# A chunked state-space scan: ScalarE makes the next chunk's first decay whole at the end of a chunk

## The reference

```
cs = cumsum(ac)                          # ac = dt * A, per head
seg = cs[:, :, None] - cs[:, None, :]
lmat = exp(where(causal, seg, -inf))     # the decay between two tokens of a chunk
cb = einsum("blgn,bsgn->blsg", cc, bc)
y_diag = einsum("blsg,blsgj,bsgjp->blgjp", cb, lmat, xc)
y_off = einsum("blgn,bgjpn,blgj->blgjp", cc, state, exp(cs))
new_state = state * exp(cs[:, -1]) + einsum("blgn,blgj,blgjp->bgjpn", bc, decay, xc)
```

## Time and profile before

| | us |
|---|---|
| median of three runs | 2900.41 (2899.1 to 2905.93) |
| the profiled execution, its own time | 2911.98 |
| its span | 2910.1 |
| busy in the span: PE / PEld | 2810.4 (97%) / 2375.7 (82%) |
| busy: DVE / ACT / POOL | 1589.1 (55%) / 1240.7 (43%) / 1583.0 (54%) |

### The profile page before, as it was taken

One profiled execution on the slowest core, in us unless ns is written; L12 is line 12 of the kernel. 1 busy time (PEld: TensorE's weight loads), 2 busy tenths in 40 slices (PEclk: granted clock), 3 DMA queues, 4 the chain that ended last, 5 costly groups with the idle time before them and its releaser, 6 DMA issues. The chain is left out here.

```text
span 2910.1 us, 40604 instructions
## 1 busy us (share of the span) xinstructions
PE 2810.4 (97%) x14222; PEld 2375.7 (82%) x14222; DVE 1589.1 (55%) x2525; ACT 1240.7 (43%) x2258; POOL 1583.0 (54%) x1078
## 2 busy tenths in 40 slices
PE   6999999999999999999998999999999988999998
PEld 5888888888877888888887788888999967788787
DVE  6335235896534346865424555555766675753433
ACT  5232234333234443332324556555767754542332
POOL 7677778777777688777763454452111244422000
PEclk8999999999999999999999999999999989999999
DMA  4557346532235265332345455554566388865543
GB/s 123 147 159 227 115 129 167 128 111 81 72 91 191 88 176 138 109 95 65 87 130 163 143 175 158 165 172 159 171 195 172 105 245 257 270 212 165 181 151 108
DMA packets 462802, 436.06 MB, mean 150 GB/s; under 512 B 60736, under 2 KB 403008, under 8 KB 454976
## 3 DMA queue, kind: packets, MB, share of 16 engines
q1 hardware_dynamic: 460352, 425.79, 49.1%
q0 software_dynamic: 2304, 8.39, 0.7%
HBM read 290.99 MB, written 143.13 MB: 149 GB/s over the span
## 5 line engine op out<-in xcount | busy, mean ns | idle before, releaser
L531 PE MATMUL p_acc<-h_kept,w_hi 128*128 128x512 f32 x1216 | 477.7, 393 | 5.0 <-ACT work L577 3.2
L533 PE MATMUL p_acc<-h_kept,w_lo 128*128 128x512 f32 x1216 | 475.5, 391 | 0.0
L532 PE MATMUL p_acc<-h_kept,w_hi 128*128 128x512 f32 x1216 | 474.2, 390 | 0.0
L417 POOL TENSOR_TENSOR w_lo<-p_sums,w_hi 128x512 fp32r<-128x512 f32 x300 | 395.2, 1332 | 136.2 <-ACT w_hi L618 136.2
L618 ACT ACTIVATE w_hi<-p_sums 128x512 fp32r<-128x512 f32 x300 | 189.3, 632 | 477.3 <-PE p_acc L533 454.8
L531 PEld LDWEIGHTS p_acc<-h_kept,w_hi 128*128 128x128 f32 x1216 | 228.9, 188 | 54.6 <-ACT work L577 3.4
L533 PEld LDWEIGHTS p_acc<-h_kept,w_lo 128*128 128x128 f32 x1216 | 228.9, 188 | 49.9
L532 PEld LDWEIGHTS p_acc<-h_kept,w_hi 128*128 128x128 f32 x1216 | 229.1, 188 | 48.6
L531 PE MATMUL p_acc<-p_ops,w_hi 128*128 128x512 f32 x608 | 241.9, 398 | 5.9 <-DVE p_ops L719 5.9
L533 PE MATMUL p_acc<-p_ops,w_lo 128*128 128x512 f32 x608 | 240.1, 395 | 0.0
L532 PE MATMUL p_acc<-p_ops,w_hi 128*128 128x512 f32 x608 | 238.3, 392 | 0.0
(11 more groups left out here) (343 smaller groups left out, 6795.3 us busy)
## 6 DMA issues: line engine op xcount, KB each, us to landing
raw<-w_in SPq DMA_DIRECT2D x100, 512.0 KB, 5.2
s_qs<-p_stage SPq DMA_DIRECT2D x96, 256.0 KB, 4.0
work<-s_gates SPq DMA_DIRECT2D x48, 512.0 KB, 7.3
p_rawb<-w_in SPq DMA_DIRECT2D x38, 512.0 KB, 4.0
keep<-w_in SPq DMA_DIRECT2D x38, 512.0 KB, 5.3
s_xbc<-p_stage SPq DMA_DIRECT2D x32, 512.0 KB, 2.6
work<-s_xbc SPq DMA_DIRECT2D x16, 1024.0 KB, 7.2
spare<-s_qs SPq DMA_DIRECT2D x16, 1024.0 KB, 6.1
```

Source lines behind the costliest of these rows:

```text
L417: tt(w_lo[:, k], weight(u, k), w_hi[:, k], ALU.subtract).then_inc(w_made, 1)
L531: pe.matmul(bank, hi, ops[k][:, 0, c], start=c == 0, stop=False)
L532: pe.matmul(bank, hi, ops[k][:, 1, c], start=False, stop=False)
L533: last = pe.matmul(bank, lo, ops[k][:, 0, c], start=False, stop=c == 3)
```

## The change

Three places in ScalarE's program. At the end of a chunk `falls` of the next chunk becomes `decays`, which is `falls` and then `decay`: the Exp of the next chunk's group 0 now stands behind its Relus and ahead of the chunk's third item. At the start of a chunk the Exp is gone. Ahead of the loop the first chunk's `falls` becomes `decays` too.

```
                         act.activation(b_tok[:], ps_m[:, :BANK], ACT.Copy).then_inc(b_tok_ready, 1)
-                        decay(c, 0)
                         decays(c, k, i, 1)
...
                         act.activation(std[:], ss[:], ACT.Sqrt, bias=eps[:], scale=1.0 / GW).then_inc(std_made, 1)
                         if not (last_pair and k):
-                            falls(c + 1, 1 - k, i + k, 0)
+                            decays(c + 1, 1 - k, i + k, 0)
                         take_item(3 * k + 2)
...
-                falls(0, 0, 0, 0)
+                decays(0, 0, 0, 0)
                 with act.Fori(0, PAIRS - 1) as i:
```

## The result

The changed kernel takes 2909.54 us (median of 22 runs, 2899.23 to 2923.8) against 2901.59 us of before in the same sessions (22 runs, 2897.55 to 2914.92): ratio 1.0022, 95% interval [1.0013, 1.0031]. It is slower by 0.22%, some 6 us (the plain difference of the two medians is 8.0), where I forecast 2 us less; the median lies above the range of 2891 to 2908.

A forecast was written before the change was run, and what follows sets the result against it. TensorE, busy 97% of the span, was taken to bound the kernel. Summing -12 + 2.0 + 1.1 + 0.5 + 6.8 gave -1.6, say -2 us: 2898 from a median of 2900.41, range 2891 to 2908.

The forecast's parts named there:

- The gain at group(0): TensorE's delay for the moved Exp goes: 7.6 us in eight chunks, 0.5 in chunk 1, 1.25 in even chunks 4 to 12.
- The mix bound by xdt: VectorE's group(0) mix, issued when cbm is done, ends 0.55 us after GpSimd's xdt, with 1 us in hand.
- Group(3): Its mix finishes before GpSimd's cast begins, so stalls in chunks 3, 4, 5, 9, 11 go: 2.7 us gained.
- Late copies: ScalarE's keep copies at odd chunks' ends, in chunks 5 to 15, come late and delay TensorE: 2.0 us lost.
- The sum without meetings: Gains of 12 us less 2.0 late copies, 1.1 late yn in chunks 12 and 14, 0.5 for chunk 0's Exp.
- The table load: At the chunk's end, Exp starts 1.30 us after load start; rival, 2.7 us switch by skill rule: 2914, chance 0.02.
- the price of a meeting: Odd chunks' yn under GpSimd's second split: two at 2.7 us, four meeting the cast alone at 0.45, less 0.4: 6.8 us.
- The edge: Odd chunks: a second cast starting under 0.8 us behind the first yn pushes the fourth yn instruction into GpSimd's subtraction.
- y + xd is drawn out: Issued earlier, inside GpSimd's first split, y + xd takes 0.3 to 0.7 us off the yn chain's slack.
- collisions in nearly all: Rival: five or six odd chunks' yn fall over the edge, 16 us in place of 6.8; +7.6, 2908 us; chance 0.18.

The follow-up runs named there:

- guard_after: The changed kernel with GpSimd's second split of odd chunks made to wait until VectorE has made yn; 2892.26 us, 0.9957 of before.
- guard_before: The kernel of before with GpSimd's second split of odd chunks made to wait until VectorE has made yn; 2900.44 us, 0.9985 of before.
- after_again: The changed kernel run once more, unedited; 2908.45 us, 1.0017 of before.
- collide_before: The kernel of before with the second split's weights transferred one item earlier and the split held until the square root, forcing it onto yn; 2921.53 us, 1.0063.
- early: The changed kernel with the next chunk's group 0 Relus and Exp moved up behind group 3's Exp; 2903.51 us, 1.0008 of before.
- early_guard: The kernel early plus GpSimd's second split waiting for yn; 2888.74 us, 0.995 of before.
- early_guard2: The kernel early_guard with the first split of each chunk also made to wait for y + xd; 2885.87 us, 0.994 of before.
- half_even: The changed kernel with the Exp kept at the end of even chunks alone, so only odd chunks begin without it; 2910.39 us, 1.0028 of before.
- half_odd: The changed kernel with the Exp kept at the end of odd chunks alone, so only even chunks begin without it; 2898.49 us, 0.9994 of before.

## Why the prediction was wrong

- The gain at group(0), 7.6 + 0.5 + 1.25 us: right. In both profiles of the changed kernel the distance from the z transposes to group(0) is 0.87 or 0.88 us in every chunk from 1 on; the sum of what it exceeded that by in before, 9.8 us, is gone.
- The mix bound by xdt, ending 0.55 us behind it: right, to the hundredth in chunk 3. The lock that the Trainium skill, "SBUF — State Buffer", section "Who interferes with whom", describes is what the traces show: in ten of the twelve profiles y + xd meets the first split's subtraction, 98 times in all; it is issued 0.04 to 1.9 us into it and ends 1.1 us behind it each time (alone it takes 1.22), while the subtraction takes 2.38 to 2.41 us however early y + xd comes.
- Group(3), 2.7 us: right where the clock is high. In the changed kernel it is on time in chunks 3, 4, 5, 9 and 11; it is late by 0.8 and 0.4 us (from group(0) to L1196) in chunks 10 and 12, each behind a meeting and its slow clock.
- Late copies, 2.0 us: right in kind, 3.8 us in guard_after.
- The sum without meetings: -12 + 2.0 + 1.1 + 0.5 = -8.4 us. guard_after less guard_before measures -8.2. That the two agree to 0.2 us is in part luck: the late copies alone were 1.8 us dearer, TensorE's waits for yn in guard_after are 2.1 us against 1.1, and the two intervals leave 4 to 5 us of room.
- The table load: it takes 1.28 us right behind the Relus, the Exp starts 1.29 behind its start, and there is no drain of 1.38 us as the Trainium skill, "ScalarE: Activation LUTs", section "What ACT_TABLE_LOAD costs", has it. That rival was rightly low. (By its own terms, +17 on -2, it comes to 2915, not 2914.)
- The step that failed is the price of a meeting in the term of 6.8 us: "2.7 us each", with "at 2.7 us I expect none" of the clock's falls. The edge is where I put it: over the same 42 chunks 14 have a distance under 0.8 us, and each of these has an excess of 2.8 us or more; the other 28 have 0.9 at most. The count was nearly right too: of the six chunks 3 to 13 I had two fall over it, and three do in either profile of the changed kernel (3, 9 and 11; 7, 9 and 13). Chunk 1, which I left where it was, escapes in the one and meets in the other. What a meeting costs was wrong. The clock falls behind 3.04 and 2.67 us in the changed kernel (not behind 2.77 in chunk 3), and behind 2.86, 2.94, 3.16 and 2.80 us in after_again; the head of the next chunk is then stretched by up to 2 us, and its group(3) can wait as well.

The price is read from the starts of L1166, over the chunk of the meeting and the next. After_again, chunks 9 and 11:

```profile
1803.32 1.04 PE L1166 MATMUL s_psx<-ident,work 128*128 128x128 f32 x8
...
1866.82 1.04 PE L1166 MATMUL s_psx<-ident,work 128*128 128x128 f32 x8
```

These two chunks take 63.5 us, where two undisturbed ones take 55.0: 8.5 us for one meeting. The other six of the two profiles cost 3.2 (chunk 3 of the changed kernel, where the clock stays) and 4.9 to 5.7. The trace of before had this price in it already. Its chunks 1 and 5 start at:

```profile
1574.83 1.04 PE L1166 MATMUL s_psx<-ident,work 128*128 128x128 f32 x8
...
1697.38 1.04 PE L1166 MATMUL s_psx<-ident,work 128*128 128x128 f32 x8
```

With chunk 3's start at 1639.65, chunks 1 and 2 take 64.8 us and chunks 3 and 4 take 57.7: 7.1 us for the meeting in chunk 1. I had read the 4.59 us of its yn and the 3.72 us of its idle, and not the length of the chunks. By the medians, in place of 6.8 us the meetings cost what guard_after and guard_before give: 16 to 19 us in the changed kernel less 3 to 4 in before, so 13 to 15.

- A smaller part of the same step: y + xd is drawn out by 0.35 to 1.2 us over its 1.23 in the odd chunks 1 to 13 of the two profiles, where I took 0.3 to 0.7.
- The time came out where the rival "collisions in nearly all" has it (2908, given a chance of 0.18), but not by its count: it had five or six of the six go over the edge at 2.7 us each, and three do, at 3.2 to 8.5. That its number fits is luck. The two things that mattered stood in my own rows: an edge with three distances within 0.2 us of it, and a clock that fell behind the one meeting in sight. I priced both as if they were settled.

What stays open: why the landings of `raw` vary by some tenths of a us from run to run, and so whether one can place them without a wait; and behind which of the idles the clock falls.

## What to carry to other kernels

A gain on one engine moves its instructions against work on another that does not move with them, here splits that start when a transfer issued long before has landed; ask of each instruction that comes earlier what now runs beside it. Where the neighbour shuts an engine out as it does here, the cost has an edge: yn's chain, with 0.8 to 0.9 us of slack, lost 2.8 to 3.9 us beyond it in the 14 meetings. Price what lies beyond the edge from the length of whole chunks, not from the idle alone. Fix the order by a wait where the held work has slack (the second split's weights are first used behind L1196 of the next chunk, some 20 us later), and the gain is kept. Look also for an idle place with the right table loaded before moving a table load.

## What the runs showed of the hardware that I had not expected

- TensorE's granted clock falls to the lower level behind idles of 1.99, 2.00 and 1.96 us in chunks 5, 7 and 11 of collide_before, and stays high behind 1.97, 1.96, 2.32 and 1.96 us in the other four. It stays high behind 3.17 us in chunk 9 of early, and behind 3.48 us in another stage of before (L2136, at 2467.44 us). The length of the idle alone does not tell.
- A slow stretch costs more than its transposes: in the changed kernel the step from the start of chunk 12 to that of chunk 13 is 29.4 us, behind chunk 11's idle, where an undisturbed chunk takes 27.5.
- Runs of the changed kernel differ by up to 25 us (2899.23 to 2923.8, 22 runs). early_guard, whose order is fixed by a wait, spreads over 7 (2885.09 to 2892.15, 6 runs), but guard_before over 9 (2894.7 to 2903.7, 11 runs) and early_guard2 over 15 (2878.65 to 2894.12, 6 runs), so the meetings are a part of the spread and not all of it. The profiles say the same: outside of the stretch from chunk 0's yn to chunk 15's the spans are 2462.5 us (half_even) to 2475.5 (half_odd).
